# First half of the output gate's contraction begun in the last memory head

## The reference

```python
proj = h @ w_in
xm, z = jnp.split(proj, [MLSTM_WIDTH], axis=-1)
...
xc = jax.nn.silu(conv + conv_b)
...
h_f = mlstm_chunkwise(q, k, v, li_f, lf_f)
h_b = flip(mlstm_chunkwise(flip(q), flip(k), flip(v), flip(li_b), flip(lf_b)))
cell = (h_f + h_b)[:, :, PAD_FRONT:].transpose(0, 2, 1, 3)
cell = rms_norm(cell, head_norm.reshape(MLSTM_HEADS, MLSTM_HEAD_V)).reshape(bsz, l, MLSTM_WIDTH)
o = jax.nn.sigmoid(xc @ w_ogate + b_ogate)
hh = o * cell.astype(xc.dtype) + skip * xc
return (hh * jax.nn.silu(z)) @ w_out
```

## Time and profile before

| | |
|---|---|
| median of three runs | 2836.97 us (2826.1 to 2838.0) |
| the profiled execution, its own time | 2827.34 us |
| its span on the core | 2825.2 us |
| granted clock of PE, mean over the span | 0.961 |
| PE busy | 2560.4 us, 91% |
| PEld busy | 2207.0 us, 78% |
| DVE busy | 1403.6 us, 50% |
| ACT busy | 923.0 us, 33% |
| POOL busy | 1134.5 us, 40% |

### The profile page before, as it was taken

The page is one execution under the profiler, slowest core; times in us unless marked ns, Lnnn a source line. Parts: engine busy times, 40 slices in busy tenths (PEclk is TensorE's granted clock), DMA queues, the critical chain, the costliest instruction groups (busy, mean ns, idle before and its releaser), DMA issues. The chain is left out here.

```text
span 2825.2 us, 41292 instructions
## 1 busy us (share of the span) xinstructions
PE 2560.4 (91%) x15638; PEld 2207.0 (78%) x15638; DVE 1403.6 (50%) x2285; ACT 923.0 (33%) x1916; POOL 1134.5 (40%) x1244
## 2 busy tenths in 40 slices
PE   6999997699997868799799999999999699999798
PEld 6988886699996657677678888877777589998587
DVE  6464444687887936322654453555555522222314
ACT  4232222633333233223322223356565400000321
POOL 3454441177775125402054544433333355552320
PEclk9999999999998889899999999999999799999899
DMA  7323333201011464444343333343432464442543
GB/s 162 113 65 106 102 106 89 56 24 47 31 39 31 74 128 153 133 158 144 115 103 129 117 144 125 132 164 125 148 121 104 175 202 136 136 136 83 195 148 149
DMA packets 268360, 328.33 MB, mean 116 GB/s; under 512 B 45300, under 2 KB 216974, under 8 KB 267030
## 3 DMA queue, kind: packets, MB, share of 16 engines
q1 hardware_dynamic: 230006, 239.09, 28.3%
q10 hardware_dynamic: 38176, 86.78, 8.3%
HBM read 212.75 MB, written 103.55 MB: 112 GB/s over the span
## 5 line engine op out<-in xcount | busy, mean ns | idle before, releaser
L1025 POOL TENSOR_TENSOR w_hi<-w_raw,ones 128x512 fp32r<-128x512 f32 (+1 forms) x232 | 274.8, 1184 | 765.4 <-PE r L1036 263.8
L1027 POOL TENSOR_TENSOR w_lo<-w_raw,w_hi 128x512 fp32r<-128x512 f32 (+1 forms) x232 | 344.8, 1486 | 18.2
L1036 PE MATMUL r<-h_lo,w_hi 128*128 128x264 f32 (+1 forms) x864 | 286.6, 332 | 0.0
L1036 PE MATMUL r<-h_hi,w_lo 128*128 128x264 f32 (+1 forms) x864 | 278.5, 322 | 0.0
L1036 PE MATMUL r<-h_hi,w_hi 128*128 128x264 f32 (+1 forms) x864 | 277.6, 321 | 0.0
L1036 PE MATMUL r<-xc_lo,w_hi 128*128 128x264 f32 (+1 forms) x768 | 248.5, 324 | 28.4 <-POOL w_lo L1027 28.4
L1036 PE MATMUL r<-xc_hi,w_lo 128*128 128x264 f32 (+1 forms) x768 | 248.9, 324 | 0.0
L1036 PE MATMUL r<-xc_hi,w_hi 128*128 128x264 f32 (+1 forms) x768 | 248.4, 323 | 0.0
L434 POOL TENSOR_TENSOR w_lo<-w_raw,w_hi 128x512 fp32r<-128x512 f32 x64 | 85.2, 1359 | 251.0 <-ACT w_hi L500 251.0
L1036 PEld LDWEIGHTS r<-xc_lo,w_hi 128*128 128x128 f32 x768 | 146.0, 190 | 41.0 <-issue 28.9
L1036 PEld LDWEIGHTS r<-h_hi,w_hi 128*128 128x128 f32 x864 | 163.0, 189 | 16.2 <-issue 2.4
(11 more groups left out here) (345 smaller groups left out, 6376.0 us busy)
## 6 DMA issues: line engine op xcount, KB each, us to landing
w_raw<-in_w_in_even SPq DMA_DIRECT2D x72, 256.0 KB, 3.0
w_raw<-in_w_in_odd SPq DMA_DIRECT2D x64, 256.0 KB, 3.4
w_raw<-in_w_ogate SPq DMA_DIRECT2D x64, 256.0 KB, 7.1
v_d<-vs ACTq DMA_DIRECT2D x8, 1152.0 KB, 4.2
us<-u_d SPq DMA_DIRECT2D x128, 65.0 KB, 2.9
xc_d<-xc ACTq DMA_DIRECT2D x8, 1040.0 KB, 6.4
qk_d<-qk ACTq DMA_DIRECT2D x16, 520.0 KB, 2.7
sz_d<-sz SPq DMA_DIRECT2D x8, 1040.0 KB, 5.2
```

The source lines that it names most:

```text
L1025: self.nc.gpsimd.tensor_tensor(hi, raw, one, ALU.mult).then_inc(self.hi_done, 1)
L1027: self.nc.gpsimd.tensor_tensor(lo, raw, hi.bitcast(F32), ALU.subtract).then_inc(self.split, 1)
L1036: ins = self.nc.tensor.matmul(bank[:, 0:n], w[:, u % self.buffers, k, :], z[:, off:off + n], start=(first and k == 0 and w is self.hi and ...
```

## The change

`odd_units` lists two more units, the first halves of output blocks 0 and 1 of the gate. `cell_slots` gives the 240 steps of z to the first seven heads, and the last head takes the two new units: none in slots 0 to 2, two steps in each of slots 3 to 10 (one k for two pieces), three in each of slots 11 to 16, and 14 steps (`tail`) among the turns after the last cell. Their operand, blocks 0 to 7 of `xc`, is written over `h`: SP loads block k into one of two buffers in `sz[1]` (`load_xc`; blocks 0 and 1 in slots 10 and 11 of the seventh head, block k in slot k of the last), ACT writes the high part (`high`) and DVE the low part (`low`) in slot k + 1. A load waits for the low part of the block two before it. ACT copies the finished half sums into `sz0` (`keep_half`). In `ogate` only blocks 8 to 15 of `xc` are loaded; it takes over the unit weights of the memory stage, so it has two split buffers instead of four, with the first halves of blocks 2 and 3 already loaded. PE begins with these, then their second halves, then the second halves of blocks 0 and 1, to which DVE adds the halves kept, and then block by block as before.

```diff
-            weights = UnitWeights(nc, sh, [2 if kind in "qk" else KC for kind, _, _ in units])
+            weights = UnitWeights(nc, sh, [2 if kind in "qk" else KC for kind, _, _ in units] + [KC] * (4 * KC - 2))
...
-        ogate(nc, a, c, d)
+            ogate(nc, a, c, d, h, weights, len(units), sz0)
...
+    for n, one in enumerate(listed):
+        fill[divmod(n * (MH - 1) * slots // len(listed), slots)].append(one)
+    for k in range(KC):
+        fill[MH - 1, O_SLOT + k] += [(zs, 0, k), (zs, 1, k)]
+    tail = [(zs, 2, k) for k in range(KC)] + [(zs + 1, p, k) for p, k in steps]
+    for k in range(O_SLOT + KC, slots):
+        fill[MH - 1, k], tail = tail[0:3], tail[3:]
...
+                def load_xc(k):
+                    if k == 0:
+                        sp.wait_ge(cz_stored[1], 16 * 3)
+                    elif k >= 2:
+                        sp.wait_ge(x_lo, k - 1)
+                    sp.dma_start(sz[1][:, k % 2, :], d["xc"][k]).then_inc(xl[k % 2], 16)
...
+                        if j == MH - 1 and 2 <= k < KC:
+                            load_xc(k)
...
+                        if j == MH - 2 and k in (10, 11):
+                            load_xc(k - 10)
...
+                    if u == ZS and p < 2:
+                        pe.wait_ge(x_lo, k + 1)
...
                 for n in range(3):
+                    for step in tail[n * len(tail) // 3:(n + 1) * len(tail) // 3]:
+                        z_step(*step)
                     turn(MH - 1, n)
...
+                def high(k):
+                    act.wait_ge(xl[k % 2], 16 * (k // 2 + 1))
+                    if k == 0:
+                        act.wait_ge(weights.piece_done, made_at(ZS - 1, NP - 1))
+                    nc.scalar.activation(h[0][:, k, :], sz[1][:, k % 2, :], ACT.Copy).then_inc(x_hi, 1)
...
+                        if j == MH - 1 and 1 <= k <= KC:
+                            high(k - 1)
...
+                def low(k):
+                    dve.wait_ge(x_hi, k + 1)
+                    v.tensor_tensor(h[1][:, k, :], sz[1][:, k % 2, :], h[0][:, k, :].bitcast(F32),
+                                    ALU.subtract).then_inc(x_lo, 1)
...
+                        if j == MH - 1 and 1 <= k <= KC:
+                            low(k - 1)
...
-    order = [(0, 0), (1, 0), (0, 1), (1, 1)] + [(o, half) for o in range(2, NO) for half in range(2)]
+    order = [(2, 0), (3, 0), (2, 1), (3, 1), (0, 1), (1, 1)] + [(o, half) for o in range(4, NO) for half in range(2)]
+    seq = [2, 3, 0, 1] + list(range(4, NO))
...
-        x = [s.sb(n, [P, 2 * KC, L], F32R) for n in ("xc_hi", "xc_lo")]
-        weights = UnitWeights(nc, s, [KC] * len(order), buffers=4)
+        x = [s.sb(n, [P, KC, L], F32R) for n in ("xc_hi", "xc_lo")]
...
+                        if n >= 2 and (half == 0 or o < 2):
+                            pe.wait_ge(read, NP * (n - 2) + p + 1)
                         for k in range(KC):
-                            step(o, half, p, k)
+                            if (o, half) == (2, 1):
+                                pe.wait_ge(x_lo, k + 1)
...
+                    if o < 2:
+                        for p, (off, m) in enumerate(PIECES):
+                            dve.wait_ge(weights.piece_done, NP * at[o, 1] + p + 1)
+                            part = sz0[:, o, off:off + m]
+                            v.tensor_tensor(part, part, reg[b][:, 512 * p:512 * p + m], ALU.add).then_inc(added, 1)
```

More of the change, by code:

```diff
@@ L1859, in odd_units @@
     count = len(units)
-    return units + [("z", i, b) for i in range(1, MH) for b in range(2)], count
+    units += [("z", i, b) for i in range(1, MH) for b in range(2)]
+    return units + [("o", MH, 0), ("o", MH, 1)], count
 KEY_STEPS = (1, 3, 20)
@@ L2165 @@
 Z_FIRST = 4
-Z_PER_HEAD = 30
+O_SLOT = 3
 def cell_slots(units):
     slots = 2 * NT - 1
[L2173 to L2185, removed]
+    steps = [(p, k) for p in range(len(PIECES)) for k in range(KC)]
+    zs = len(units) - 2
+    fill = {(j, k): [] for j in range(MH) for k in range(slots)}
+    listed = [(u, p, k) for u in range(Z_FIRST, zs) for p, k in steps]
+    for n, one in enumerate(listed):
[5 more added lines that the diff above has]
+        fill[MH - 1, k], tail = tail[0:3], tail[3:]
+    ends = {}
+    for (j, k), several in fill.items():
+        for u, p, kt in several:
+            if kt == KC - 1:
+                ends[u, p] = (j, k)
     later = {}
@@ L2188, in cell_slots @@
         later.setdefault((j, k + 1) if k + 1 < slots else (j + 1, 0), []).append((u, p))
-    return fill, ends, later
+    return fill, ends, later, tail
 def mlstm_z(nc, a, c, d, h, weights, units, first, hs, raw, sz0):
@@ L2201, in mlstm_z @@
     SLOTS = 2 * NT - 1
-    fill, ends_at, evicted_in = cell_slots(units)
+    fill, ends_at, evicted_in, tail = cell_slots(units)
+    ZS = len(units) - 2
     GROUPS = [range(0, 3), range(3, 6), range(6, 9)]
@@ L2248, in mlstm_z @@
         win = a["w_in_odd"].rearrange("(k p) n -> p k n", p=P)
+        wog = a["w_ogate"].rearrange("(k p) n -> p k n", p=P)
+        xl, x_hi, x_lo = [s.sem(f"x_loaded{b}") for b in range(2)], s.sem("x_hi_done"), s.sem("x_lo_done")
+        o_read = s.sem("o_read")
         def made_at(u, p):
@@ L2262, in bank, with slot @@
             return hp[:, at:at + 512]
-        split_in = {}
-        for u in range(Z_FIRST + 2, len(units)):
-            j, k = after(u - 2)
-            for part in range(2):
[L2268 to L2274, removed]
+        def slot(u, more):
+            j, k = after(u)
+            return divmod(j * SLOTS + k + more, SLOTS)
+        split_in, load_in, stored_in = {}, {}, {}
+        for u in range(Z_FIRST + 2, ZS + 3):
+            for part in range(2):
+                split_in[slot(u - 2, part)] = (u, part)
+        for u in range(Z_FIRST + 4, ZS + 4):
+            load_in[slot(u - 4, 2)] = u
+        for u in range(Z_FIRST, ZS):
             if units[u][2] == 1:
-                j, k = after(u)
-                stored_in[(j, k + 1)] = head_of(u)
+                stored_in[slot(u, 1)] = head_of(u)
         with nc.Block() as block:
@@ L2763, in _ @@
                 for u, (o, half) in enumerate(order):
-                    weights.load(sp, u, wog[half, :, :, o * P:(o + 1) * P])
+                    if u >= 2:
+                        weights.load(sp, first + u, wog[half, :, :, o * P:(o + 1) * P])
                     if half == 1:
-                        operands(o)
+                        operands(seq.index(o))
             @block.gpsimd
             def _(gp):
-                for u in range(len(order)):
+                for u in range(1, len(order)):
@@ L2771, in _ @@
                     for part in range(2):
-                        weights.split_half(gp, u, part, c["ones"])
+                        weights.split_half(gp, first + u, part, c["ones"])
             @block.tensor
             def _(pe):
-                def step(o, half, p, k):
-                    if half == 0 and k == 0 and o >= 2:
-                        pe.wait_ge(read, NP * (o - 2) + p + 1)
-                    if o < 2:
-                        pe.wait_ge(x_lo, half * KC + k + 1)
-                    weights.step(pe, at[o, half], p, k, reg[o % 2][:, 512 * p:512 * p + 512],
-                                 lambda k: (x[0][:, half * KC + k, :], x[1][:, half * KC + k, :]),
-                                 first=(half == 0), last=(half == 1))
@@ L2805, in _ @@
[L2805 to L2811 removed]
+                for k in range(KC):
+                    act.dma_start(buf[:, k, :], d["xc"][KC + k]).then_inc(xl[k], 16)
```

98 lines of the change are left out of this document (58 added, 40 removed).

## The result

The changed kernel takes 2813.63 us (median of 4 runs, 2812.82 to 2817.63), the kernel before beside it 2834.6 us: a ratio of 0.9933, 95% interval [0.9908, 0.9958]. A later run of the same two on one chip gave 2811.64 us against 2829.59, 0.9929 [0.9909, 0.9948]. The profiled execution takes 2813.59 us (span 2811.8), 13.4 us less in span than the one before.

What follows compares the result with a forecast made beforehand. PE was taken to set the time in memory heads and gate. Gate and hand-over -41.4, heads 0 to 6 +10.7, last head +16.0 sum to -14.7 us: 2812.6 or 2822.3 by base, predicted 2818, range 2800 to 2840.

Steps and rivals of the forecast that it cites:

- Forecast A: Whole kernel: a gain of 8 to 22 us, 2805 to 2829 over both bases; chance 50%.
- the two bases: Starting times for the sum: profiled execution 2827.34 us, giving 2812.6, and three-run median 2836.97, giving 2822.3.
- Gate and hand-over: Last cell to the gate's end: 367.1 us instead of 408.5, a gain of 41.4 us.
- rival D: Gate: two split buffers instead of four become PE's limit; kernel 16 us slower, 2843 to 2853; chance 10%.
- Heads 0 to 6: First seven memory heads: 240 steps of z instead of 210 cost 10.7 us, at most 14.3.
- I take one step of 4.3 as absorbed: Heads 0 to 6: of 4.3 extra steps each, one falls into a wait; 7 x 3.2 x 0.476 = 10.7 us.
- The last head: Last memory head: a loss of 16 us, with ends of +4 and +27, from refilling h and more steps.
- block 2's landing: Last head's refill: block 2, queued behind the store of z, lands at +12.4 us; near +10.5 without that wait.
- fill and clock: Last head, PE's slots 9 to 16: 22 steps instead of 15 cost +1.5 us; a low clock at restart +1.5.
- the chain's pace: Last head's refill through two buffers: 6.6 us per pair of blocks, of which the load 3.7; scores 13 us late.
- Rivals B and C: B: refill hidden, last head loses only 5 us, 2801 to 2811, 18%. C: gain all paid back, 2827 to 2837, 22%.

Runs made afterwards that it cites:

- experiment 1: Changed kernel, with weight splits in a head's first five slots made to wait until DVE has scaled the head before: 2811.59 us, 0.9946 of the kernel before.
- experiment 9: Kernel of experiments 8, with the last head's refill copies and subtractions moved out of slots 6 and 7: 2800.91 us, 0.9887 of the kernel before.
- experiment 2: Kernel before, with four weight splits held until the next head's root is done, when DVE starts to scale: 2846.68 us, 1.0062 of the kernel before.
- experiments 8: Changed kernel; splits in heads 2 and 4 after scalings, seven refill buffers, z store behind their loads, six left-over steps behind last turn: 2800.14 us, 0.9889 of before.

## Why the prediction was right, and where its steps were not

- **Forecast A**, a gain, came in: 2813.63 for 2818 predicted. On the profiled executions the sum was -14.7 and the difference -13.4. Its base was the weak point: the three runs shown had a median of 2836.97, later ones of the kernel before 2828 to 2831, so the profiled execution was the better base. 2818 was a mean of the two bases; on the later medians the same sum gives 2813 to 2816.
- **Gate and hand-over**: from the last cell to the gate's end 366.4 us, predicted 367.1. The turns ended at +13.1 (14.6), the gate began at +20.5 (22.2) and lasted 345.9 (344.9), its half clock at the start costing some 3 us instead of 2. Two buffers held nothing up, so rival D is out: no wait in 30 units.
- **Heads 0 to 6**: +11.8 measured, +10.7 predicted, and nearly right by luck: heads 1, 3, 5 and 6 took 0.2 to 1.0 us more each, heads 2 and 4 3.5 and 5.9, where 1.5 each was said. The failed step is "I take one step of 4.3 as absorbed". With the splits moved (experiment 1), heads 1 to 6 together take 5.4 us more than before, 0.9 each where 1.5 was said: more than half of the steps fall into waits. The other 6.3 us in heads 2 and 4 are a cost that the sum had no term for. The plan moved POOL's split as well, since a split is let go by the end of the unit two before; I counted PE's steps and did not ask what else the moved ends set off. The kernel before had such a collision in head 3, whose third group of scalings took 3.57 us. That group stands behind the addition of PE's long wait; PE waited only 0.41 us for the next one, and the head took 47.40:

```profile
1979.28 3.57 DVE L2633 TENSOR_SCALAR hs<-hs,rstd 128x256 f32<-128x256 f32 x3
```
```profile
1983.45 0.67 PE L2371 MATMUL ub<-v__307,kw 128*128 128x257 f32 x2 [0.41 <-DVEq L2604]
```

- **What I should have weighed.** The Trainium skill, "SBUF — State Buffer", section "Who interferes with whom", says that a GpSimd instruction and a VectorE one in a two-port mode, which tensor_scalar can enter, exclude each other for a whole instruction. The trace agrees: 0.88 us became 3.36, while an addition that reads one operand from PSUM took 0.47 beside the same split.
- **The last head**: +14.9, predicted +16.0, and block 2's landing at +12.4 as worked out (+10.5 was worked out for a load that passes the store). The store of z, issued at +1.75, landed 9.4 us later, at about +11, ahead of the load. By the rule that the prediction cited from the Trainium skill, "DMA: Bandwidth & Descriptors", section "Queues, rings and completion order" (one ring, taken in order), the load follows the store; the trace agrees. Mis-sized were the shares: the refill costs 9.2 us, not 13, and the steps with the empty first slots 5.7, not the 1.5 and 1.5 set for fill and clock; the two errors nearly cancelled, which is luck. What I took for the chain's pace, the loads, was only part of it: they held blocks 2 to 5, and with every load in time the head still takes 57.8 us. What holds it then, DVE's order, PE's half clock at the head's start or both, stays open: experiment 9 did not settle which of DVE's operations to move.
- **Rivals B and C.** The last head lost neither 5 us nor 27. PE did not stay at 1.2 GHz from slot 3 on either: it had 1.00 of the clock in the midst of the refill, with waits of 0.60 and 0.89 us in this stretch, and again behind it:

```profile
2188.12:2196.12 8.00, 5.54 (x31) 3.89 (x29) 6.28 (x9) 4.88 (x8) 0.00 (x0) 1.00 0.55 192
2204.12:2212.12 8.00, 8.00 (x45) 7.10 (x44) 4.07 (x13) 4.88 (x16) 2.85 (x4) 1.00 0.00 1
```

- **Not explained** is the rest between the medians: -18 and -21 us, against -15.4 by the stages of the two profiles. The start of the heads, ahead of the change, moves by up to 12 us between executions.

## What to carry to other kernels

When a plan moves work on one engine, list everything that is released by the moved ends, on the other engines too: here a weight split on GpSimd landed on VectorE's scalings and cost 6.3 us, nearly half of the 14.3 that all of the extra steps could have cost. A term that comes out right is no proof of its reason; a table of stage lengths head by head would have shown at once that two heads of seven carried the loss. And what is left over at a stage's end belongs behind the last thing that another engine waits for, not ahead of it.

## What the runs showed of the hardware

- Beside GpSimd's splits three VectorE scalings of 128 x 256 took 3.36 and 3.37 us instead of 0.88, in the changed kernel and in that of experiment 2; GpSimd's own instructions kept their 1.04 and 1.26.
- The same short wait costs clock in one execution and not in another. In head 1 of experiments 8 and 9, whose code for that head is the same, PE waits 1.29 us at the first scores; then:

```profile
1904.50 0.49 PE L2412 MATMUL kq<-qk 128*128 128x128 f32 x2 [1.29 <-DVE sw L2778]
...
1904.95 0.29 PE L1036 MATMUL z<-h_hi,w_hi 128*128 128x264 f32 x1
```
```profile
1904.89 0.72 PE L2413 MATMUL kq<-qk 128*128 128x128 f32 x2 [1.29 <-DVE sw L2780]
...
1905.62 0.42 PE L1036 MATMUL z<-h_hi,w_hi 128*128 128x264 f32 x1
```

The second, of experiment 9, runs its next matmuls at the lower level (0.50 of the clock over the 3 us behind 1905.0, 1.00 over those behind 1904.7 in the first), and its head took 48.47 us against 46.92. A single head's length is therefore known to some 1.5 us from one profile (head 0 less well still: 41.98 and 44.72 us in two executions of the changed kernel), and differences under that between two kernels mean little.
